# Query product first, and the compressed branch laid between the key-value tiles

## What is computed

```python
def compress(kv_raw, pe, w1, w2):
    idx = jnp.arange(n_cmp)[:, None] * D_CMP + jnp.arange(L_CMP)[None, :]     # 31 windows of 32 rows, step 16
    blocks = kv_raw[:, idx] + pe[None, None, :, None, :]
    blocks = blocks.transpose(0, 1, 3, 2, 4).reshape(bsz, n_cmp, N_KV_GROUPS, L_CMP * HEAD_DIM)
    return jax.nn.silu(blocks @ w1) @ w2

kv = (rms_norm(h, kv_norm) @ w_kv).reshape(bsz, seq, 6, 4, 64)
k_cmp, v_cmp = compress(kv[:, :, 0], pe_k, w1_k, w2_k), compress(kv[:, :, 1], pe_v, w1_v, w2_v)
qg = rms_norm(h, b_norm) @ w_qg                       # queries and gates
s = q @ k_cmp - slopes * (t - cmp_center)             # compressed branch
p_cmp = softmax(where(vis, s, NEG_INF)) * vis
o_cmp = p_cmp @ v_cmp
...                                                   # two more branches over kv[:, :, 2:4] and kv[:, :, 4:6]
o = gate0 * o_cmp + gate1 * o_slc + gate2 * o_win
```

## Time and profile before

| | us |
|---|---|
| median of three runs | 2256.83 |
| lowest and highest | 2255.29, 2257.19 |
| the profiled execution | 2257.51 |
| its span, first to last instruction | 2255.7 |
| mean granted TensorE clock | 0.975 |

### The profile page before, as it was taken

One profiled execution on the slowest core, in us unless ns is written; L12 is line 12 of the kernel. 1 busy time (PEld: TensorE's weight loads), 2 busy tenths in 40 slices (PEclk: granted clock), 3 DMA queues, 4 the chain that ended last, 5 costly groups with the idle time before them and its releaser, 6 DMA issues.

```text
span 2255.7 us, 25561 instructions
## 1 busy us (share of the span) xinstructions
PE 2145.8 (95%) x9956; PEld 1696.7 (75%) x9956; DVE 1143.6 (51%) x1735; ACT 750.6 (33%) x1113; POOL 770.8 (34%) x198
## 2 busy tenths in 40 slices
PE   7999999999978788999999989999999998999999
PEld 6888888888867334688888867776678876888887
DVE  5545873662143688568548444466664745110121
ACT  4123222223222577432122244454453423221221
POOL 3444444434422111144344342212222133444433
PEclk9999999999988799999999999999999999999999
DMA  4223434422351000134243131211112122223322
GB/s 162 93 95 138 159 112 149 149 84 87 109 174 56 1 1 1 57 131 149 103 177 131 59 116 56 75 38 57 57 38 75 38 75 75 93 79 108 105 79 96
DMA packets 34203, 205.03 MB, mean 91 GB/s; under 512 B 4160, under 2 KB 5312, under 8 KB 14784
## 3 DMA queue, kind: packets, MB, share of 16 engines
q1 hardware_dynamic: 31968, 196.84, 24.8%
q10 hardware_dynamic: 2144, 6.95, 1.0%
HBM read 199.58 MB, written 2.10 MB: 89 GB/s over the span
## 4 chain that ended last, share of the span: by engine, by line
PE 86%; DVE 7%; ACT 4%; issue 2%; POOL 0%; DMA 0%; ACTq 0%; SPq 0%; DVEq 0%; POOLq 0%
PE PS L502 22%; PE PS L503 22%; PE PS L504 22%; PE PS L798 3%; PE PS L800 2%; PE PS L799 2%; PE PS L712 1%; PE PS L700 1%; PE PS L687 1%; ACT PB L1259 1%; ACT PT L1268 1%; PE PS L878 1%; PE PS L846 1%; DVE SPH L1522 1%; PE PS L840 1%
## 5 line engine op out<-in xcount | busy, mean ns | idle before, releaser
L442 POOL TENSOR_TENSOR WL<-WR,WH 128x2048 fp32r<-128x2048 f32 (+2 forms) x173 | 739.0, 4272 | 1322.2 <-ACT WH L1072 1322.2
L502 PE MATMUL PS<-Hh,WH 128*128 128x512 f32 x1632 | 644.7, 395 | 22.9 <-DVE Hl L1568 11.1
L503 PE MATMUL PS<-Hl,WH 128*128 128x512 f32 x1632 | 639.0, 392 | 0.0
L504 PE MATMUL PS<-Hh,WL 128*128 128x512 f32 x1632 | 638.6, 391 | 0.0
L1072 ACT ACTIVATE WH<-WR 128x2048 fp32r<-128x2048 f32 (+2 forms) x173 | 305.5, 1766 | 727.7 <-PE PS L504 719.1
L502 PEld LDWEIGHTS PS<-Hh,WH 128*128 128x128 f32 x1632 | 309.1, 189 | 92.5 <-issue 23.1
L503 PEld LDWEIGHTS PS<-Hl,WH 128*128 128x128 f32 x1632 | 309.1, 189 | 65.9 <-issue 2.2
L504 PEld LDWEIGHTS PS<-Hh,WL 128*128 128x128 f32 x1632 | 308.7, 189 | 64.8
L502 PE MATMUL PS<-Gh,WH 128*128 128x512 f32 x592 | 232.4, 393 | 0.0
L503 PE MATMUL PS<-Gl,WH 128*128 128x512 f32 x592 | 231.9, 392 | 0.0
L504 PE MATMUL PS<-Gh,WL 128*128 128x512 f32 x592 | 231.7, 391 | 0.0
(11 more groups left out here) (271 smaller groups left out, 2333.4 us busy)
## 6 DMA issues: line engine op xcount, KB each, us to landing
WR<-wA SPq DMA_DIRECT2D x125, 1024.0 KB, 4.8
AW<-wada SPq DMA_DIRECT2D x24, 1024.0 KB, 5.6
WR<-wB SPq DMA_DIRECT2D x24, 768.0 KB, 4.1
WR<-wC SPq DMA_DIRECT2D x24, 640.0 KB, 3.8
X<-x_in SPq DMA_DIRECT2D x8, 256.0 KB, 6.6
W1K<-w1k ACTq DMA_DIRECT2D x1, 2048.0 KB, 9.7
W1V<-w1v ACTq DMA_DIRECT2D x1, 2048.0 KB, 14.9
out<-X SPq DMA_DIRECT2D x8, 256.0 KB, 4.6
```

The source lines that it names most:

```text
L442: nc.gpsimd.tensor_tensor(WL[:, s, 0:n], WR[:, s, 0:n], WH[:, s, 0:n].bitcast(F32), ALU.subtract).then_inc(lo_s, 1)
L502: nc.tensor.matmul(PS[:, b, :], wh[:, c, cols], pe_h, start=c == 0, stop=False)
L503: nc.tensor.matmul(PS[:, b, :], wh[:, c, cols], pe_l, start=False, stop=False)
L504: last = nc.tensor.matmul(PS[:, b, :], wl[:, c, cols], pe_h, start=False, stop=c == seg.chunks - 1)
```

## The change

The segments `wq` and `wkv` change places, in the weights and in the program, and with them the gains with which `Hh` and `Hl` are written. The gates' product runs after the fourth query tile. The key-value tiles use two banks and are cut into quarters of 6 matmuls, and the compressed branch stands between the quarters. PE multiplies `W1` by windows read in place from `RW` (every 16th token); the position term becomes a bias of the activation, made by DVE (`bias_sum`) and a product with ones (`bias_products`). The raw rows of keys are copied by DMA after tile 1 and those of values after tile 3. `OC`, `XO` and `XJ` are gone: the compressed products open the accumulation of each pair in `values`. POOL's first two `BIAS` tiles no longer wait for a compressed output.

```diff
-    ("wkv", "A", 6), ("wq", "A", 4), ("wo", "A", 4),
+    ("wq", "A", 4), ("wkv", "A", 6), ("wo", "A", 4),
@@ GpSimd
-                pool.wait_ge(dist_s, 32)
-                pool.wait_ge(oc_s, DC)
-                for pair in range(DC):
+                for pair in pairs:
+                    if pair == 0:
+                        pool.wait_ge(dist_s, 16)
+                        pool.wait_ge(vt_t, 2)
+                    if pair == 1:
+                        pool.wait_ge(vt_t, 4)
...
-                    body(0)
-                    distances()
+                    body(0, 0, 1)
+                    distances((0,))
+                    body(0, 1)
+                    distances(range(1, DC))
@@ TensorE
+            def quarter(name, t, j, xh=Hh, xl=Hl, bank=None):
...
+                if j == 0:
+                    if m == 0:
+                        pe.wait_ge(lo_s, seg.unit0 + t // 2 + 1)
+                    pe.wait_ge(evac_s, seg.tile0 + t - 1)
...
+                first_unit("wkv", h_ready)
+                tile(2, 0, 1, 2, 3)
+                hidden_rows(0, 0)
+                tile(3, 0, 1)
+                hidden_rows(0, 4)
...
+                tile(4, 2, 3)
+                bias_products()
+                hidden_rows(1, 0)
...
                 if j0 == 0:
                     pe.wait_ge(w1_s[s], 16)
-                pe.wait_ge(xj_s, 4 * s + j0 // 4 + 1)
+                    pe.wait_ge(rw_s[s], 128)
...
-                        mm = nc.tensor.matmul(PS[:, 4 + 2 * s + mc, 0:4 * CG], W1[s][:, j, mc * P:mc * P + P],
-                                              XJ[:, s, j, :, :].rearrange("p g n -> p (g n)"),
+                        mm = nc.tensor.matmul(out, W1[s][:, j, mc * P:mc * P + P],
+                                              RW[s][:, :, 2 * j:2 * j + 16 * (NCMP - 1) + 1:16],
                                               start=j == 0, stop=j == 15)
...
+            def bias_products():
+                pe.wait_ge(bs_s, 2)
...
+                    if br == 0 and kb == 0:
+                        j = pair % 4
+                        for hf in range(2):
+                            g = 2 * (pair // 4) + hf
+                            nc.tensor.matmul(PS[HD * hf:HD * hf + HD, pair % 2, :], VC[CG * j:CG * j + CG, g, :],
+                                             PCT[CG * j:CG * j + CG, g, :], start=True, stop=False)
@@ ScalarE
+            def load_rows(s):
+                act.wait_ge(evac_s, SEGS["wkv"].tile0 + 2 * s + 2)
+                for g in range(4):
+                    src = KV[HD * (g % 2):HD * (g % 2) + HD, 2 * s + g // 2, :]
+                    act.dma_start(RW[s][0:HD, g, :], src).then_inc(rw_s[s], 16)
+                    act.dma_start(RW[s][HD:P, g, 0:T - 1], src[:, 1:T]).then_inc(rw_s[s], 16)
...
+                hi(wkv.unit0 + 2)
+                load_rows(0)
+                hi(wkv.unit0 + 3)
+                load_rows(1)
+                act.wait_ge(hb_t, 1)
@@ VectorE
+            def bias_sum(s):
+                dve.wait_ge(w1_s[s], 16)
+                acc = BSUM[:, s, :]
+                for j in range(16):
+                    w, pe_col = W1[s][:, j, :], pcol("pek" if s == 0 else "pev", j)
+                    if j == 0:
+                        ins = nc.vector.tensor_scalar(acc, w, pe_col, None, ALU.mult)
+                    else:
+                        ins = nc.vector.scalar_tensor_tensor(acc, w, pe_col, acc, ALU.mult, ALU.add)
...
+                keys_values(1)
+                bias_sum(0)
+                keys_values(2)
+                bias_sum(1)
+                keys_values(3)
...
-                    chain.mark(nc.vector.tensor_tensor(XO[:, :], OC[:, pair, :], PS[:, pair % 2, :], ALU.add))
-                    chain.wait()
-                    split(Hh[:, pair, :], Hl[:, pair, :], XO[:, :], o_s)
+                    split(Hh[:, pair, :], Hl[:, pair, :], PS[:, pair % 2, :], o_s)
```

More of the change, by code:

```diff
@@ L515, in dense @@
                 if only is not None:
-                    body(only, ready is not None)
+                    body(only, ready is not None, used)
                     return
@@ L675, in attention, with keys_product @@
-            def attention():
-                pe.wait_ge(oc_s, DC)
+                    for mc in range(2):
+                        mm = nc.tensor.matmul(PS[:, 7, 2 * s + mc:2 * s + mc + 1], BSUM[:, s, mc * P:mc * P + P],
+                                              ones[:, 0:1], start=True, stop=True)
+                mm.then_inc(hb_t, 1)
+            def keys_product():
+                pe.wait_ge(hid_s, 2)
+                w2 = pcol("w2k", 0, 256).rearrange("p (c m) -> p c m", c=2)
+                out = PS[:, 6, 0:4 * CG].rearrange("p (g n) -> p g n", g=4)[:, :, 0:NCMP]
+                for mc in range(2):
+                    mm = nc.tensor.matmul(out, w2[:, mc, :], HID[:, mc, :, 0:NCMP], start=mc == 0, stop=mc == 1)
+                mm.then_inc(kvc_t, 1)
@@ new lines, in values_product @@
+            def values_product():
+                pe.wait_ge(hid_s, 4)
+                pe.wait_ge(hz_s, 1)
+                w2 = pcol("w2v", 0, 128).rearrange("p (c m) -> p c m", c=2)
+                for g in range(4):
+                    for mc in range(2):
+                        rows = HIDR[:, mc, g, :, :].rearrange("p r n -> p (r n)")
+                        mm = nc.tensor.matmul(PS[:, 7, g * HD:(g + 1) * HD], rows, w2[:, mc, :],
+                                              start=mc == 0, stop=mc == 1)
+                mm.then_inc(kvc_t, 1)
@@ new lines, in compressed_scores @@
+            def compressed_scores(qb):
+                if qb == 0:
+                    pe.wait_ge(kvc_s, 2)
+                if qb >= 2:
+                    pe.wait_ge(sc_m, qb - 1)
+                for pair in range(DC):
+                    a, j = pair // 4, pair % 4
+                    o = PS[:, 2 + qb % 2, 2 * P * a:2 * P * a + 2 * P].rearrange("p (b x) -> p b x", b=2)
+                    mm = nc.tensor.matmul(o[:, :, j * CG:j * CG + CG], QT[:, pair, qb * P:qb * P + P],
+                                          KC[:, a, :, :], start=True, stop=True)
+                mm.then_inc(sc_t, 1)
@@ L680, in score_pair, with turn_compressed, attention @@
+            def turn_compressed(qb):
+                pe.wait_ge(sc_n, qb + 1)
+                if qb:
+                    pe.wait_ge(pc_s, qb)
+                for g in range(4):
+                    mm = nc.tensor.transpose(PS[:, 4, g * P:g * P + P], SE[:, qb % 2, g * P:g * P + P], ident[:, :])
+                mm.then_inc(pc_t, 1)
+            def attention():
+                pe.wait_ge(pc_s, QB)
+                pe.wait_ge(vt_s, 3)
                 def score_pair(p):
@@ L2197 @@
     ff(f_gu[0][:, :F], f_gu[0][:, F:], f_dn[0])
-    kinds["A"].append(units(tiles(a["w_kv"]), 2))
     order = [8 * p + j + 4 * h for p in range(2) for j in range(4) for h in range(2)]
```

468 lines of the change are left out of this document (237 added, 231 removed).

## The result

| | before | after |
|---|---|---|
| median of five runs, us | 2255.29 | 2242.52 |
| lowest and highest | 2254.51, 2257.19 | 2240.84, 2247.0 |
| span of the profiled execution | 2255.7 | 2238.9 |
| mean granted TensorE clock | 0.975 | 0.981 |

The ratio is 0.994, with a 95% interval of 0.9928 to 0.9952. The kernel is 0.6% faster, 13 us by the medians. The forecast was 2225, a gain of 32. The time lies half a microsecond inside the stated range (2210 to 2243) and far from the forecast.

What follows compares the result with a forecast made beforehand. Bound: PE's work plus, in two places, chains of small steps with PE otherwise idle. Work 50.3 + 93.3, stalls 11.0, clock 2.5 make 157.1 against 190.0; 2257.5 - 32.9 + 0.8 (attention) = 2225.4, so 2225 us; range 2210 to 2243.

Steps and rivals of the forecast that it cites:

- Query part: Eight query tiles 43.5, gates' product 5.4, norm's sum 0.9, gates' turn 0.45: 50.3 us, other engines' steps costed at nothing.
- PE's work in the key-value part: Twelve tiles, eight `hidden_rows` blocks at 1.7 each, scores, small products and turns at full clock: 93.3 us.
- the other end that the text had named (14): Operand read in place: nothing taken; at the slowest traced rate 1.8 us more for each of eight blocks, 14.
- The large wait, 6.7: PE waits for the raw values' DMAs, because tile 3's copy stands behind the second bias sum on DVE: 6.7 us.
- 6.7 + 1.2 + 2.5: Key-value part: wait for raw values' DMAs 6.7, wait for the bias 1.2, half clock after a gap 2.5 us.
- Small waits: Key-value part: tile 2 waits 1.1 us for tile 0's bank; PE waits 2.0 us for the raw keys' DMAs.
- Attention, +0.8 forecast: Attention over the pairs: 0.8 us longer in all, between 4 shorter and 7 longer.
- The start: Start of attention: gain of 1 us at a higher clock, though POOL's step may hold DVE for 3 us.
- half of 8 x 1.0 as a loss: Attention pairs: compressed products cost PE 1.0 us each, half counted; half of 8 x 0.42 gained on DVE; net 2.
- the late compressed chain: Key-value part: turns wait for the compressed chain as before, so the second soft place's gain is lost; 2242, chance 0.05.
- The doubled operand: `hidden_rows`: strided operand at double time, or two more DVE collisions, gives 2235 to 2239; joint chance 0.19 for 2231 to 2243.
- the signs of being wrong that were named: `hidden_rows` blocks clearly over 1.8 us, waits before the turns, clock under 0.9 across the stretch, or a pair over 1 us longer.

Runs made afterwards that it cites:

- lo_late: The changed kernel with only GpSimd's second low part of `wo` moved behind the third pair's `BIAS`; 2238.22 us, ratio 0.992.
- the steps run: The changed kernel with the eight `hidden_rows` blocks reading at steps 1, 2, 4, 8, 16, 3, 12, 6 (wrong tokens); 2240.91 us in one run.
- the run with sorted rows: The changed kernel with raw keys and values written sorted, so `hidden_rows` reads four runs of 31 neighbouring values; 2238.38 us, ratio 0.9915.

## Why the prediction was off, point by point

The profiled span missed the forecast by some 15 us. Attention has 9.9 of them, the rewritten stretch 3.4 and the part behind attention 2.0.

- Query part: 50.3 forecast, 50.6 measured. Right, with nothing exposed.
- PE's work in the key-value part: the first step that failed is "The nearest row is DVE's copy of the very same windows ... so I take nothing". The stepped operand cost 1.5 a block, 12 us in all, near the other end that the text had named (14). A row of another engine was taken for the nearest. The Trainium skill's sentence on lines (SBUF — State Buffer, Door 1: The DMA port swizzle), which the prediction set aside, is borne out for PE: 3.2 us a block for 1.7. It is not for DVE's copy, 315 ns.
- The large wait, 6.7: right in mechanism and size (6.18) for a PE that comes as early as the sum had it, and absent in the kernel as changed. PE came to the first values' block at 657.9, where the sum had it at 652.1 (612.6 + 39.5), and tile 3's copy ended at 646.2, where the sum had 651.9. The doubled blocks and the wait hid each other: 12 us of work replaced 6.7 + 1.2 + 2.5 = 10.4 of forecast wait and clock. That is why the stretch was missed by only 3 us, and it is luck: the sum looks nearly right and is wrong in two terms.
- Small waits: tile 2, 1.1 forecast, 0.29 idle shown; raw keys 2.0 forecast, 1.71 shown, with some 3 us at half clock behind it that the forecast did not have (1.1 us, 634.77 to 638.61 for two quarters that cost 2.7 at full clock).
- Attention, +0.8 forecast, +10.7 measured: the second step that failed, and the larger one. The start: a gain of 1 was taken, a loss of 2.3 came (19.33 for 17.07). The prediction had named POOL's step on the first scalings and 3 us of hold, then netted it against the higher clock. But with that hold PE waited 5.20 us, against 1.96 in `lo_late`. The higher clock did not last: it fell to half in both, for some 10 us with the hold and some 7 without. The pairs: "half of 8 x 1.0 as a loss" was mis-sized, the products cost 1.0 each in full; the addition gave back 0.45 a pair, all of the 0.42 that was taken by half. From the third `BIAS` step to the eighth the pairs took 108.2 us against 101.9: some 3 us for the products net of the addition (21.03 against 20.03 and 20.47), and 3 us for two falls of the clock, a term that the forecast did not have and whose cause is open. The last stretch, to the output product, took 2.1 more.
- The rivals: the late compressed chain said 2242, which is the measured time, but by luck. No turn waited; between 631.49 and 722.56 PE has no idle of over 0.25 us. The doubled operand said 2235 to 2239 and is the nearest in mechanism. It added its price to the forecast's waits, and left attention alone.
- Of the signs of being wrong that were named, two came: blocks of over 1.8 us, which pointed at the operand, and two of five pairs longer than before by over 1 us, which were the ones with a fall of the clock. None pointed at the start of attention.

## What to carry to other kernels

When a change reads an operand of TensorE in place instead of from a packed copy, price it on TensorE: in float32 at double time when neighbouring columns lie 16 bytes or more apart, as measured here up to 64 bytes; if nothing in the trace has such an operand, put that price in the forecast and not in the range. When a stage becomes longer or shorter, walk again through who arrives when: here a slower PE removed a wait and a faster one restored it. Packing the operand gave 2.7 us in the key-value part, and moving one copy ahead of one sum, once it was packed, another 8.6. And look at where GpSimd's long steps fall after a reorder, beside which of VectorE's short ones.

## What the runs showed of the hardware

- TensorE's time for a float32 product with 124 columns depends on the step between columns: 1.7 to 1.8 us for eight products at 1 or 2 values, 2.6 at 3, 3.3 to 3.4 at 4, 6, 8, 12 and 16. Between 16 and 64 bytes the distance made no difference.
- The stepped block costs nothing more at half clock. At step 16 it took 3.38 us in the steps run, at a granted clock of 0.57, and 3.28 in the kernel after, at 1.00 (657.86 to 661.14). A packed block took 3.40 at 0.50 in the run with sorted rows (659.05 to 662.45) and 1.70 at full clock.
- A running GpSimd step of 4.5 us holds a VectorE scaling from SBUF to SBUF until it ends (two of them took 3.85 us, and 0.61 without it). Cut in four, it held the two scalings for one piece each (1.17 and 1.30 us each, with pieces of 1.26).
- Behind TensorE's wait for the raw keys, 1.7 to 2.1 us long in full work, the granted clock fell to half for some 3 us in eight traces of nine; in the steps run, with a wait of 1.69 us, it did not. Inside attention, short falls appeared in every changed kernel, at places that differed from one execution to the next, with PE at 86% busy (154.58 of 180.68 us) where it was 86% before too (124.21 of 145.00).
